# Gate pre-activations of an mLSTM layer in four column tiles of TensorE, their partial sums added by a fold matrix

## The reference

```python
xm, z = up[..., :A_INNER], up[..., A_INNER:]
...
xc = jax.nn.silu(xconv)
...
q = _headwise(xc, w_q)
k = _headwise(xc, w_k)
v = _headwise(xm, w_v)
gates = (jnp.concatenate([q, k, v], axis=-1) @ w_if + b_if).astype(f32)
ig = jnp.transpose(gates[..., :A_HEADS], (0, 2, 1))
lf = jnp.transpose(jax.nn.log_sigmoid(gates[..., A_HEADS:]), (0, 2, 1))
```

## Time and profile before

| | us |
|---|---|
| median of 3 runs | 1763.48 |
| lowest and highest | 1763.22, 1764.52 |
| profiled execution | 1764.59 |
| its span, first to last instruction | 1762.60 |
| TensorE busy in the span | 1609.9 (91%) |
| VectorE, ScalarE, GpSimd busy | 665.3, 389.7, 221.7 |
| mean granted TensorE clock | 0.944 |

### The profile page before, as it was taken

The page is one execution under the profiler, slowest core; times in us unless marked ns, Lnnn a source line. Parts: engine busy times, 40 slices in busy tenths (PEclk is TensorE's granted clock), DMA queues, the critical chain, the costliest instruction groups (busy, mean ns, idle before and its releaser), DMA issues. The chain is left out here.

```text
span 1762.6 us, 22229 instructions
## 1 busy us (share of the span) xinstructions
PE 1609.9 (91%) x8553; PEld 1084.1 (62%) x8553; DVE 665.3 (38%) x1418; ACT 389.7 (22%) x916; POOL 221.7 (13%) x293
## 2 busy tenths in 40 slices
PE   6998598989898699997995999999899999999987
PEld 5886264646464598443444998894347775477752
DVE  1542225555454731005113222032205762176624
ACT  3211131313141321004002221210003331133202
POOL 4010040303030000000003110000201112011120
PEclk9998888989999799998997999959999999999999
DMA  5110027474747622123824240021312211222011
GB/s 161 56 41 0 5 90 244 149 256 145 250 159 242 233 96 103 56 95 125 264 73 135 88 138 1 5 96 48 94 59 97 73 30 52 92 77 77 3 67 51
DMA packets 92639, 181.89 MB, mean 103 GB/s; under 512 B 9927, under 2 KB 23907, under 8 KB 91331
## 3 DMA queue, kind: packets, MB, share of 16 engines
q1 hardware_dynamic: 89286, 163.76, 27.6%
q0 software_dynamic: 3248, 16.72, 2.9%
HBM read 133.82 MB, written 54.95 MB: 107 GB/s over the span
## 5 line engine op out<-in xcount | busy, mean ns | idle before, releaser
L1112 PE MATMUL ps<-wring,xnT 128*128 128x512 f32 (+2 forms) x464 | 177.9, 546 | 0.0
L1112 PEld LDWEIGHTS ps<-wring,xnT 128*128 128x128 f32 (+1 forms) x464 | 83.3, 196 | 97.0 <-issue 96.9
L347 PE MATMUL ps<-xnT,wring 128*128 128x288 f32 (+1 forms) x512 | 120.6, 397 | 1.2 <-PEq L2395 1.2
L1112 PE MATMUL ps<-wring,xcT 128*128 128x512 f32 x256 | 110.9, 594 | 0.0
L347 PEld LDWEIGHTS ps<-xnT,wring 128*128 128x128 f32 x512 | 98.0, 193 | 20.9 <-ACT xnT L268 1.3
L884 DVE SCALAR_TENSOR_TENSOR wring<-wring,nbw,ps 128x512 f32<-128x512 f32 x128 | 86.7, 742 | 63.3 <-PE ps L635 62.1
L2033 ACT ACTIVATE P<-ps,nmx 128x128 f32<-128x128 f32 (+3 forms) x128 | 67.3, 527 | 168.1 <-DVE nmx L2057 167.1
L1932 PE MATMUL ps<-KT,Qp 128*128 128x128 f32 (+3 forms) x256 | 96.5, 459 | 0.0
L2057 DVE TENSOR_REDUCE nmx<-ps 128x1 f32<-128x128 f32 (+3 forms) x128 | 62.0, 486 | 85.2 <-PE ps L1933 84.9
L1112 PEld LDWEIGHTS ps<-wring,xcT 128*128 128x128 f32 x256 | 48.3, 190 | 62.6 <-issue 62.6
L1997 PE MATMUL ps<-V,PT 128*128 128x64 f32 x640 | 85.1, 265 | 0.0
(11 more groups left out here) (434 smaller groups left out, 2755.7 us busy)
## 6 DMA issues: line engine op xcount, KB each, us to landing
wring<-in_state_C_dram SPq DMA_DIRECT2D x32, 1024.0 KB, 6.0
out_dram<-wring SPq DMA_DIRECT2D x32, 1024.0 KB, 5.6
wring<-in_a_w_up_dram SPq DMA_DIRECT2D x8, 2048.0 KB, 8.9
wring<-in_b_w_in_dram SPq DMA_DIRECT2D x8, 2048.0 KB, 8.2
wring<-in_a_w_down_dram SPq DMA_DIRECT2D x4, 2048.0 KB, 7.8
craw<-in_cache_kv_dram SPq DMA_DIRECT2D x64, 128.0 KB
arena<-in_cache_kv_dram SPq DMA_DIRECT2D x32, 256.0 KB, 3.8
arena<-in_cache_win_dram SPq DMA_DIRECT2D x8, 1024.0 KB, 4.9
```

The costliest lines, as they stand in the source:

```text
L347: m = pe.matmul(b[:, 0:t1 - t0], w[:, kt, 128 * m4:128 * m4 + 128], k.xnT[:, kt, t0:t1], start=kt == 0, stop=kt == KD - 1)
L1112: m = pe.matmul(b[0:n, 0:w.shape[2]], xT[:, 8 * half + kt, 128 * i:128 * i + n], w[:, kt, :], start=half == 0 and kt == 0, stop=half == ha ...
```

## The change

Each tile f of wc gets 32 columns of which the first eight hold the gates, side by side, so that one copy in place of two moves a part into wc. The matmuls of tile f write to the column group 32 * (f % 4) of a bank (key parts): all 16 tiles of xm first, then all 16 of xcT, for the first half and then the second. Each group ends up with the sum of four f. VectorE copies the 128 partitions of this bank into the new tile parts in SBUF, and two matmuls with columns 0 to 3 and 4 to 7 of fold add the four groups and put the input gates at partitions 0 to 3 and the forget gates at 32 to 35 of another bank (key gate), where the bias additions read them as before.

```diff
--- before.py
+++ after.py
@@ -292,7 +292,8 @@
     convt = sb("convt", [128, 2, XPW])
     bdt = sb("bdt", [128, 3, FT // 4, 128])
     nraw = sb("nraw", [128, 128])
-    wc = sb("wc", [128, 2 * FT, 36])
+    wc = sb("wc", [128, 2 * FT, 32])
+    parts = sb("parts", [128, TA])
     tails = sb("tails", [128, FT, 27])
     tail_rows = crow
     block = ctx.enter_context(nc.Block())
@@ -353,21 +354,25 @@
         for r in range(4):
             drained(pe, k, ("wc", r))
         for hf, (t0, t1) in enumerate(HALF):
-            b, full = open_bank(pe, k, ("gate", hf))
-            pe.wait_ge(k.xc_ready, 1)
-            pe.matmul(b[0:36, 0:t1 - t0], wc[:, 0, :], k.xcT[:, 0, t0:t1], start=True, stop=False)
+            b, full = open_bank(pe, k, ("parts", hf))
             for f in range(FT):
-                if hf == 0:
-                    pe.matmul(b[0:36, 0:256], wc[:, FT + f, :], k.xp[:, f, 3:259], start=False, stop=False)
-                else:
-                    pe.matmul(b[0:36, 0:256], wc[:, FT + f, :], k.xp[:, f, 259:515], start=False, stop=False)
-                    pe.matmul(b[0:36, 256:288].rearrange("p (b i) -> p b i", i=SI), wc[:, FT + f, :],
+                p0 = 32 * (f % 4)
+                x0 = 3 + 256 * hf
+                pe.matmul(b[p0:p0 + 32, 0:256], wc[:, FT + f, :], k.xp[:, f, x0:x0 + 256], start=f < 4, stop=False)
+                if hf:
+                    pe.matmul(b[p0:p0 + 32, 256:288].rearrange("p (b i) -> p b i", i=SI), wc[:, FT + f, :],
                               k.xs[:, f, :, 3:7], start=False, stop=False)
-            for f in range(1, FT):
+            for f in range(FT):
+                p0 = 32 * (f % 4)
                 if hf == 0:
                     pe.wait_ge(k.xc_ready, f + 1)
-                m = pe.matmul(b[0:36, 0:t1 - t0], wc[:, f, :], k.xcT[:, f, t0:t1], start=False, stop=f == FT - 1)
+                m = pe.matmul(b[p0:p0 + 32, 0:t1 - t0], wc[:, f, :], k.xcT[:, f, t0:t1], start=False, stop=f >= FT - 4)
             m.then_inc(full, 1)
+        for hf, (t0, t1) in enumerate(HALF):
+            drained(pe, k, ("parts", hf))
+            b, full = open_bank(pe, k, ("gate", hf))
+            pe.matmul(b[0:4, 0:t1 - t0], k.fold[:, 0:4], parts[:, t0:t1], start=True, stop=True)
+            pe.matmul(b[32:36, 0:t1 - t0], k.fold[:, 4:8], parts[:, t0:t1], start=True, stop=True).then_inc(full, 1)
         pe.wait_ge(k.tails_ready, 2)
         for r in range(4):
             b, full = open_bank(pe, k, ("tail", r))
@@ -457,9 +462,7 @@
             b, free = full_bank(dve, k, ("wc", r))
             for part in range(2):
                 src = b[:, 32 * part:32 * part + 32].rearrange("p (g j) -> p g j", j=8)
-                rows = wc[:, FT * part + q4 * r:FT * part + q4 * r + q4, :]
-                dve.tensor_copy(rows[:, :, 0:4], src[:, :, 0:4])
-                m = dve.tensor_copy(rows[:, :, 32:36], src[:, :, 4:8])
+                m = dve.tensor_copy(wc[:, FT * part + q4 * r:FT * part + q4 * r + q4, 0:8], src)
             m.then_inc(free, 1)
         for f in range(FT):
             conv(f)
@@ -469,6 +472,9 @@
                 keep_gate_weights(f // 4 - 1)
         keep_gate_weights(3)
         dve.wait_ge(k.bif_here, 32)
+        for hf, (t0, t1) in enumerate(HALF):
+            b, free = full_bank(dve, k, ("parts", hf))
+            dve.tensor_copy(parts[:, t0:t1], b[:, 0:t1 - t0]).then_inc(free, 1)
         for hf, (t0, t1) in enumerate(HALF):
             b, free = full_bank(dve, k, ("gate", hf))
             dve.tensor_scalar(k.gates[:, 0, t0:t1], b[0:4, 0:t1 - t0], k.bif[0:4, :], None, ALU.add)
```

## The result

The changed kernel takes 1743.11 us in the median of 4 runs (1741.99 to 1744.57), the kernel before 1763.35 beside it (1762.79 to 1764.52, 4 runs): a ratio of 0.9886, 95% interval 0.9871 to 0.9902, 20.2 us. The forecast was 1742.7 in 1740.8 to 1749.2.

A forecast was written before the change was run, and what follows sets the result against it. TensorE, busy 91% of the span, was taken to bound the kernel, with nothing hiding the gate stage's length. Savings of 0.16 + 10.24 + 11.87 less 1.47 gave 20.8 us, so 1742.7 us, range 1740.8 to 1749.2.

The forecast's parts named there:

- Four groups side by side: Gate matmuls: four pieces in four column groups take the time of one; 10.24 us saved in first half, 11.87 in second.
- The first half: 32 gate matmuls of 256 columns: 16.44 us before, 6.20 after, with the clock rising at 171.2 us.
- The alternating part: Second half, 16 matmuls of 256 columns alternating with 16 of 32: four rounds of four f, 1.97 us.
- the first rival: Alternating matmuls go tile by tile, 7.39 us; second half saves 6.45, total 1748.1 us; chance 0.20, including half way to it.
- The copies of wc: In front of the first gate matmul: two of the last four copies go, 0.16 us saved.
- The fold: Behind the last partial-sum matmul: copy, fold pairs and four bias additions lengthen the path, 1.47 us lost.
- t + 1.46: Kernel before: end of the two bias additions, counted from t, the start of the last partial-sum piece.
- the sum for L1418: 32 column-tiled matmuls elsewhere in the trace, used for the pace: 4 x 0.427 + 11 x 0.216 + 0.38 = 4.47 us.
- Nothing lost or gained elsewhere: Behind the gate stage: its gain enters the span one to one; same length from state_C loads to the end.
- The other rivals: Whole change: low clock 1750.0 us (0.08), no overlap 1764.8 (0.03), array drained at each tile change 1771.2 (0.02).
- The low clock: Gate stage: column tiles fail to raise the clock from 1.2 GHz; 13.5 us saved, total 1750.0 us; chance 0.08.
- A price for a change of tile: Partial-sum matmuls: each tile change drains the array, 0.10 us each, 6.4 us; total 1771.2 us, slower; chance 0.02.

The follow-up runs named there:

- one_tile: Changed kernel with all gate matmuls in column group 0 and the fold over 32 partitions; 1765.05 us, ratio 1.0014 to the kernel before.
- two_tiles: Changed kernel with two column groups (f modulo 2) and the fold over 64 partitions; 1750.54 us, ratio 0.9930 to the kernel before.
- after_again: Second profile of the changed kernel, unedited, run again on another occasion; 1743.48 us, ratio 0.9880 to the kernel before.
- runs2: Changed kernel with two 256-column matmuls in a row per column group, alternating part left as it was; 1741.31 us, ratio 0.9876 to the kernel before.
- split128: Changed kernel with each 256-column matmul of the alternating part issued as two of 128 columns; 1745.35 us, ratio 0.9897 to the kernel before.
- runs8: Changed kernel with all eight matmuls of a group in a row (twelve in the second half); 1759.16 us, ratio 0.9974 to the kernel before.
- no_fold: Changed kernel without partial-sum copies and fold matmuls, so the sum over the four groups is left out; 1739.32 us, ratio 0.9866 to the kernel before.
- runs4: Changed kernel with f reordered so four matmuls in a row go to one column group; 1752.43 us, ratio 0.9942 to the kernel before.

## Why the prediction was right

**Four groups side by side.** Shown by one_tile, two_tiles and the pieces in fours. The first half took 5.21 us, forecast 6.20. The term that was off is the clock: the changed kernel's gate stage began at 166.51 and not 165.62, the clock rose at 170.2 and not 171.2, and so the stage had 1.2 GHz for 3.7 us and not 5.6. The windows (busy us of PE, PEld, DVE, ACT, POOL, then granted clock, DMA):

```profile
166.50:170.20 3.70, 3.69 (x36) 2.02 (x40) 0.00 (x0) 0.00 (x0) 0.00 (x0) 0.52 0.02 4
170.20:175.90 5.70, 5.70 (x132) 4.19 (x124) 0.42 (x1) 0.00 (x0) 0.00 (x0) 1.00 0.01 3
```

With 3.7 us at 0.427 a group and the rest at 0.216, 8.7 + 7.3 groups make 5.3. Where the rise falls differs from execution to execution: in after_again the clock is 0.50 from 169.4 to 175.0, 5.6 us, and the first half takes 6.23; runs2, with the same work, has 6.18. The forecast had taken over the instant of the kernel before, for which no run gives a reason. The shifting rise probably makes part of the 2.6 us over which the four runs spread; a profile of each run would be needed to show it.

**The alternating part.** It took 1.99 us, forecast 1.97, and the first rival's 7.39 did not come. But the reason that I gave, that each group works through its own list whatever stands between, is only half of it, and I had said that the row did not show it for three waiting pieces. The runs put the most at three: a 256-column and a 32-column matmul on one group are one piece running and three waiting. With one matmul more per f the part would have doubled, as in split128, and with twelve in a row the groups would have met only at their ends (27.4 us for the stage in runs8). The forecast was right with no room to spare, and as to that limit by luck. The rule of the Trainium skill ("TensorE: Matmul & The Clock Gate", Part 3, What overlaps and what doesn't), that matmuls start in program order and loads overlap only across row groups, does not hold between column groups within this limit. The trace has eight loads within 0.23 us at 166.48, and in split128 a matmul of the next group starts at 172.55, ahead of the last one of the group before it (172.77). Beyond the limit the pieces behind do wait (2.62 us a group in runs8).

**The copies of wc.** 0.29 us for two, where four took 0.41; 0.12 less, forecast 0.16. The first gate matmul did not come earlier for it but 0.73 us later, by what lies ahead (the result's table).

**The fold.** 1.38 us more from the last matmul to the last addition (2.44 less 1.06; 2.43 in after_again), forecast 1.47; no_fold confirms it. (By the forecast's own terms its t + 1.46 is t + 1.47, and the sum for L1418 is 4.46 and not 4.47; neither matters.) The chain is the one forecast: the copy at 175.93, the second fold pair at 176.44 with 0.17 us of waiting, hidden under the first-half additions at 176.31.

**Nothing lost or gained elsewhere.** From the last addition to state_C 0.15 us more. It holds one thing that I had not costed: the clock falls in the middle of the tails' transposes (granted clock 0.71 over 179.20 to 181.82), which take 2.59 us for 1.93. In after_again it does not (1.00, 1.93 us), so this too is the execution and not the change. The rest of the span is 0.9 us shorter, no more than between two executions of one kernel (1539.3 before; 1538.4 and 1536.7 in two profiles of the changed kernel).

**How close the total came.** The terms add up to 20.8 us; the profiled pair differs by 21.8 (1764.59 and 1742.78) and the medians by 20.2. So the sum is right to 1 us, and most of that is the clock. That the forecast of 1742.7 lies only 0.4 us from the median is luck: the runs of one kernel differ by more.

**The other rivals.** The low clock did not come (1.00 from 170.2 to the end of the matmuls). A price for a change of tile would have shown in two_tiles, which changes as often and took 8.04 us of the expected 8.0, and in runs2, which changes half as often outside the alternating part and took 4.18 us for the second half like the changed kernel; neither shows one.

## What to carry to other kernels

Where matmuls have 32 or fewer output columns and a sum over many tiles, spreading them over the four column groups can divide their time by up to four (second half here: 15.96 us to 4.17), for the price of a copy and a small fold on the path (here 1.4 us); here TensorE alone was the limit of the stage, so all of it was gained. Change the group with every matmul or every second one: an f32 matmul is two pieces, and a fourth waiting piece in one group holds up all others. And look at what follows the last result: moving the tails away from behind these gates was worth about half as much as the change, and needed only another place in the program.

## What was not expected of the hardware

- TensorE lets other column groups go on while three pieces wait in one, and not four: with 8, 16 and 6 pieces in a row on one group the next group began with the fifth, the thirteenth and the third piece (runs4, runs8, split128). Whether it is three pieces or the loads and products of which they consist, these runs don't tell apart, since each piece had a load of its own. That a fourth is too many is read from when the next group began; no run has exactly four waiting, since the pieces come in twos.
- Four groups each reading moving data of their own, 256 columns of 128 partitions, keep the pace of one: 0.216 us a piece at 2.4 GHz in both.
